# A streaming encoder step on one core: token parts stored straight and read with a stride of eight, the last scatter cut in two, and three waits loosened

## The chip, the cores and the metric

The kernel runs on one core of one Trainium2 chip. A time is the device time of one execution in microseconds (us). The core has TensorE (PE; its loads of stationary operands are shown as PEld), VectorE (DVE), ScalarE (ACT), GpSimd (POOL) and SyncE (SP), which issues most of the DMAs. Each engine works through its own list in order and meets the others at semaphores.

## The reference, cut to what matters

One step of a trunk of two layers, for 256 prompt tokens and 32 new tokens (288 in all) of 1024 features. Of a layer, this change touches the ends and the expert part:

```
z = x @ w_in                                   # rnn stream, q, k, v, two gates
...                                            # recurrence, banded attention, merge
x = LayerNorm(alpha * x + merged @ w_out)
eidx, gate = _route(x2, w_router, e_bias)      # 8 of 64 experts for each token
shared = (silu(x2 @ ws1) * (x2 @ ws3)) @ ws2
ff = shared + sum over chosen experts of gate * (silu(x2 @ w1[e]) * (x2 @ w3[e])) @ w2[e]
x = LayerNorm(alpha * x + ff)
```

Everything is in float32.

## The kernel before

Activations lie transposed in `xT` (feature on the partition, 8 chunks `c` or `k` of 128 features, 288 tokens along the row). Tokens in rows lie in `tok` (three tiles `t` of 128, 128 and 32 tokens, 1024 features along the row). Weights stream in pieces of 1 MB through the ring `dense` (three places); for most of them ACT stores a rounded high part (`high_parts`, fp32r) and DVE the remainder (`low_parts`), and PE adds three products (`over_parts`).

**Start.** SP loads the identity, the tokens, the other constants (743 KB, `consts_in`) and then the first pieces; POOL loads the cached keys and values at once. PE turns the tokens (`fill_xT`, L578 and L581), ACT and DVE copy the chunks to `xT` (even chunks ACT, odd ones DVE, counted by `z_free`), PE turns the tables of small vectors and cached keys (L612, L613), DVE keeps them (L1275 to L1287), ACT takes an exponential (L1026). Only then the first columns of `z` follow (`over_features`, L551, columns m = 0 and 1 in plain float32, then `over_parts` for m = 2 on). PE waits for all eight chunks of `xT` ahead of the first of them, in both layers (L623).

**Router.** After the first LayerNorm PE turns the rows back (L578), ACT and DVE apply scale and shift on the way to `xT` (`norm_back`, L1019 and L1378), PE makes the router's logits (L797), DVE copies them (L1575), PE turns them (L801), and a long chain of small DVE instructions picks the experts (`sel`, L1610). Between these, the token rows are split for the gather: ACT stores the rounded part `xh` (`keep_high`, L1162), DVE the remainder `xl` (`keep_low`, L1568). Both are written in another order than `tok` has: feature f*8+k goes to place k*128+f, so that the gather reads 128 neighbouring words.

**Experts.** They are taken four at a time, a quad, 16 quads a layer, in two halves `u`. `gather` (L849, L850, L852) makes the tokens of a quad into columns: for each chunk k it takes 128 features of `xh` or `xl` as the stationary operand and the one-hot matrix `oh` (256 columns) as the moving one. `up` is L867, `turn` L875, `slots_to_tokens` L896, `down` L887. `combine` (L908, L909) scatters the results back to the tokens, 8 chunks c, each over both halves u; the chunks rotate through the four PSUM banks `SWAP`, and DVE adds each to `ffT` (`add_output`, L1668), which frees its bank. The scatter of a quad runs inside the next quad; that of the last quad has nothing to run in and follows its `down`. Then come three matmuls that only keep the clock up (`keep_clock(2, 3)`, L599), a read of the number of rounds (L946), the turn of `ffT` into rows (`to_tokens`, L586) and the second LayerNorm (`stats` on DVE, L1333; `norm_rows` on ACT, L1010).

A second round of quads would run if an expert had more than 64 tokens; it is skipped here.

The lines that set the reading order of the gather's stationary operand, and the order of the store:

```python
x = slice(k * P, k * P + P)                                        # L842
mm(o, xh[:, t, x], oh[:, t, :], start=t == 0, stop=False)          # L849
activation(xh[0:n, t, :].rearrange("p (k f) -> p f k", k=KC),      # L1162
           tok[0:n, t, :].rearrange("p (f k) -> p f k", k=KC), ACT.Copy)
```

## Time and profile before

| | us |
|---|---|
| median of 3 runs | 1642.45 |
| lowest and highest | 1642.26, 1644.33 |
| the profiled execution | 1643.55 |
| its span in the trace | 1641.7 |
| mean granted TensorE clock in it | 0.992 |

The page gives the busy time of each engine over the span. In 40 equal slices TensorE is at 9 tenths in nearly all of them, the granted clock is 9 or more in all, and the DMA engines are busy for 9 tenths in the slices of the expert part. Below, a row of the timeline reads: start in us from the span's beginning, duration in us (of all instructions of the row), engine, line, operation, written tile and read tiles, shapes, count, and in brackets the idle time ahead of it with what ended it.

### The profile page before, as it was taken

Reading aid. Unit: us, or ns where it says so; the run is one execution under the profiler, and the core shown is the slowest. Engines: PE = TensorE matmul, PEld = TensorE weight load, DVE = VectorE, ACT = ScalarE, POOL = GpSimd, SP = SyncE. Lnnn points to the kernel's source line nnn. Section 1 sums busy time; section 2 is a strip of 40 time slices with the busy share of each in tenths; the row PEclk is TensorE's granted clock in tenths of the full one; section 3 lists DMA queues with packets and bytes.
Section 4 is the critical chain, followed back from the end, with each engine's and each line's share of the span. In section 5 each row is a group of like instructions: output and inputs, shape, how many; then the busy total and the mean of one; then the engine's idle time right before and its main releaser. Section 6 shows DMA issues by size and latency. Waiting matters only on the chain.

```text
span 1641.7 us, 25658 instructions
## 1 busy us (share of the span) xinstructions
PE 1588.7 (97%) x9526; PEld 1050.1 (64%) x9526; DVE 742.4 (45%) x1525; ACT 575.6 (35%) x1138; POOL 23.0 (1%) x38
## 2 busy tenths in 40 slices
PE   7989998999999999999999999989999999999997
PEld 6968997655554555545588789965545555455553
DVE  5568666333323423333464786562333332342335
ACT  4756533232232223223157564342223223222222
POOL 2000000000000000000010000000000000000000
PEclk9999999999999999999999999999999999999999
DMA  7553356399999999999435534457999999999980
GB/s 203 187 185 120 109 174 237 144 369 405 405 391 404 406 391 410 391 401 401 161 105 173 201 104 136 154 205 282 390 403 397 399 401 390 411 394 399 404 355 30
DMA packets 141556, 477.35 MB, mean 291 GB/s; under 512 B 10020, under 2 KB 74084, under 8 KB 108724
## 3 DMA queue, kind: packets, MB, share of 16 engines
q1 hardware_dynamic: 139728, 473.50, 74.7%
q0 software_dynamic: 1408, 2.85, 0.7%
q8 instruction: 42, 0.69, 0.2%
q14 instruction: 22, 0.18, 0.0%
q10 hardware_dynamic: 356, 0.13, 0.0%
HBM read 474.88 MB, written 1.57 MB: 290 GB/s over the span
## 4 chain that ended last, share of the span: by engine, by line
PE 93%; DVE 3%; ACT 1%; issue 1%; DMA 1%; SPq 0%; DVEq 0%; ACTq 0%
PE ps L867 27%; PE ps L887 14%; PE ps L551 7%; PE ps L564 6%; PE ps L566 6%; PE ps L565 6%; PE ps L908 5%; PE ps L909 4%; PE ps L849 4%; PE ps L850 4%; PE ps L852 2%; PE ps L896 1%; PE ps L829 1%; PE ps L875 1%; PE ps L651 1%
## 5 line engine op out<-in xcount | busy, mean ns | idle before, releaser
L867 PE MATMUL ps<-experts,xg 128*64 128x512 f32 x2048 | 450.5, 592 | 0.0
L867 PEld LDWEIGHTS ps<-experts,xg 128*64 128x64 f32 x2048 | 147.5, 137 | 290.9 <-issue 290.1
L887 PE MATMUL ps<-experts,hidT 128*64 128x512 f32 x1024 | 233.8, 598 | 1.8 <-ACT hidT L1200 1.8
L564 PE MATMUL ps<-parts 128*128 128x288 f32 x736 | 222.7, 303 | 0.3
L566 PE MATMUL ps<-parts,dense_lo 128*128 128x288 f32 x736 | 216.6, 294 | 0.0
L1649 DVE TENSOR_TENSOR hid<-ps,hid 128x256 f32<-128x256 f32 x64 | 27.2, 425 | 385.5 <-ACT hid L1194 385.5
L1208 ACT ACTIVATE yh<-ps,gsl 128x512 fp32r<-128x512 f32 x128 | 88.0, 687 | 228.2 <-PE ps L887 228.2
L1194 ACT ACTIVATE hid<-ps 128x256 f32<-128x256 f32 x64 | 24.6, 384 | 397.6 <-PE ps L867 397.6
L1661 DVE SCALAR_TENSOR_TENSOR yl<-ps,gsl,yh 128x512 fp32r<-128x512 f32 x128 | 96.1, 751 | 124.5 <-ACT yh L1208 124.5
L1186 ACT ACTIVATE xg<-ps,gperm_all 128x256 f32<-128x256 f32 x256 | 130.6, 560 | 61.2 <-PE ps L852 57.6
L908 PE MATMUL ps<-ohT,yh 128*128 128x288 f32 x512 | 145.1, 308 | 3.1 <-DVE yl L1661 3.1
L887 PEld LDWEIGHTS ps<-experts,hidT 128*64 128x64 f32 x1024 | 68.5, 136 | 121.6 <-issue 121.6
L564 PEld LDWEIGHTS ps<-parts 128*128 128x128 f32 x736 | 138.1, 188 | 3.7 <-issue 2.0
L909 PE MATMUL ps<-ohT,yl 128*128 128x288 f32 x512 | 139.9, 297 | 0.0
L849 PE MATMUL ps<-oh,xh 128*128 128x256 f32 x512 | 139.3, 294 | 0.0
L566 PEld LDWEIGHTS ps<-parts,dense_lo 128*128 128x128 f32 x736 | 138.5, 188 | 0.0
L850 PE MATMUL ps<-oh,xl 128*128 128x256 f32 x512 | 133.2, 282 | 0.0
L551 PE MATMUL ps<-xT,dense 128*128 128x288 f32 x480 | 128.0, 427 | 3.0 <-ACT xT L1019 1.8
L1668 DVE TENSOR_TENSOR ffT<-ps,ffT 128x288 f32<-128x288 f32 x256 | 115.5, 457 | 24.9 <-PE ps L909 10.5
L1326 DVE TENSOR_TENSOR dense_lo<-dense,parts 128x1024 fp32r<-128x1024 f32 x92 | 108.4, 1220 | 24.7 <-ACT parts L995 24.7
L908 PEld LDWEIGHTS ps<-ohT,yh 128*128 128x128 f32 x512 | 96.2, 188 | 29.2 <-issue 24.3
L551 PEld LDWEIGHTS ps<-xT,dense 128*128 128x128 f32 x480 | 94.9, 200 | 30.9 <-issue 2.1
(275 smaller groups left out, 2022.5 us busy)
## 6 DMA issues: line engine op xcount, KB each, us to landing
experts<-in_w SPq DMA_DIRECT2D x384, 1024.0 KB, 9.6
dense<-in_w_in SPq DMA_DIRECT2D x34, 1024.0 KB, 5.5
dense<-in_w_br_rnn SPq DMA_DIRECT2D x8, 1024.0 KB, 5.3
dense<-in_w_br_attn SPq DMA_DIRECT2D x8, 1024.0 KB, 5.2
dense<-in_w_out SPq DMA_DIRECT2D x8, 1024.0 KB, 5.4
dense<-in_ws SPq DMA_DIRECT2D x6, 1024.0 KB, 5.5
tok<-in_x_prompt SPq DMA_DIRECT2D x1, 1024.0 KB, 5.9
out_y_prompt<-tok SPq DMA_DIRECT2D x2, 512.0 KB, 2.6
```

Source lines behind the costliest of these rows:

```text
L551: last = mm(bank[:, 0:n], w[:, k, col:col + P], rhs(k), start=k == 0, stop=k == KC - 1)
L564: mm(bank[:, 0:T], w_hi[:, k, col:col + P], hi[:, k, :], start=k == 0, stop=False)
L566: last = mm(bank[:, 0:T], w_lo[:, k, col:col + P], hi[:, k, :], start=False, stop=k == KC - 1)
L849: mm(o, xh[:, t, x], oh[:, t, :], start=t == 0, stop=False)
L850: mm(o, xl[:, t, x], oh[:, t, :], start=False, stop=False)
L867: last = mm(ps[e % 2 * CAP:(e % 2 + 1) * CAP, 2, :], xg[:, k, e * CAP:e * CAP + CAP], experts[:, e, 0:2, k * DE:k * DE + DE], start=k == 0 ...
L887: last = mm(ps[e % 2 * CAP:(e % 2 + 1) * CAP, 3 + b, :], hidT[:, m, e % 2 * CAP:(e % 2 + 1) * CAP], experts[:, e, 2, m * D + b * 512:m * D ...
L908: mm(o, yh[:, u, c * P:c * P + P], ohT[:, u, :], start=u == 0, stop=False)
L909: last = mm(o, yl[:, u, c * P:c * P + P], ohT[:, u, :], start=False, stop=u == 1)
L1186: last = activation(xg[:, k, :], ps[:, SWAP[j], k % 2 * 256:k % 2 * 256 + 256], ACT.Identity, bias=gperm_all[:, L, 1, k:k + 1], scale=gper ...
L1326: V.tensor_tensor(low[:, x], slot[:, x], as_f(whi[:, f % 2, x]), ALU.subtract).then_inc(wlo_ready, 1)
L1668: V.tensor_tensor(ffT[:, c, :], ps[:, SWAP[c % len(SWAP)], 0:T], ffT[:, c, :], ALU.add).then_inc(c_added, 1)
```

## The change

Five things:

1. **Stores and reads of the split token rows.** `xh` and `xl` are stored in the order of `tok`; the gather takes every eighth word of a row as its stationary operand, `slice(k, D, KC)`.
2. **Router stage.** DVE itself stores `xh` of tile 0 and its remainder ahead of `norm_back`; the remainders of tiles 1 and 2 are taken after the gate values and after the first one-hot matrix. `oh` moves in memory, so that it doesn't lie on `tok`.
3. **Last quad.** Its scatter is cut: half 0 runs in that quad, where another quad has its gather (chunks 0 to 3 ahead of `turn`, 4 to 7 behind it), half 1 after its `down`. DVE adds 8 + 8 chunks in place of 8. The three matmuls that kept the clock are gone, and the number of rounds is read ahead of the last quad. `to_tokens` starts when four chunks are added.
4. **Start.** The other constants are loaded behind the first weight piece, POOL's loads wait for the tokens, and the tables are turned after columns m = 0 and 1.
5. **First columns of `z`, both layers.** PE waits chunk by chunk for `xT`.

```diff
@@ SP, POOL
-            sp.dma_start(cst[:, P:NCONST], inp["consts"][:, P:NCONST]).then_inc(consts_in, 16)
...
                     load_piece(L, d)
+                    if L == 0 and d == 0:
+                        sp.dma_start(cst[:, P:NCONST], inp["consts"][:, P:NCONST]).then_inc(consts_in, 16)
...
+            pool.wait_ge(x_in, 32)
@@ PE
+                def xk_filled(k):
+                    pe.wait_ge(z_free[k % 2], Z_FIRST + L * Z_HALF - KC // 2 + k // 2 + 1)
+                    return xT[:, k, :]
...
-                        over_features(bank_of(L, Z_RNN + m), D_IN, m % 2 * P, xk, T).then_inc(z_ready[m % 2], 1)
+                        over_features(bank_of(L, Z_RNN + m), D_IN, m % 2 * P, xk if m else xk_filled, T).then_inc(z_ready[m % 2], 1)
+                        if L == 0 and m == 1:
+                            turn_tables()
...
-                            x = slice(k * P, k * P + P)
+                            x = slice(k, D, KC)
...
+                def combine_first(n, cs):
...
+                    for c in cs:
+                        if c < len(SWAP):
+                            pe.wait_ge(c_added, FREE + n * KC)
+                        else:
+                            pe.wait_ge(first_half_added, before + (c - len(SWAP) + 1))
+                        combine_half(0, c).then_inc(first_half_full, 1)
...
                     up(n, 1)
-                    if not last:
+                    if last:
+                        combine_first(n, range(0, 4))
+                    else:
                         gather(n + 1, n, range(2))
                     turn(n, 1)
-                    if not last:
+                    if last:
+                        combine_first(n, range(4, KC))
+                    else:
                         gather(n + 1, n, range(2, 4))
...
-                keep_clock(2, 3)
...
-                to_tokens(ffT)
+                n = pe.snap(done)
+                combine_second(n)
+                to_tokens(ffT, lambda h: pe.wait_ge(c_added, FREE + n * KC + 4 * (h + 1)))
@@ ACT
-                    activation(xh[0:n, t, :].rearrange("p (k f) -> p f k", k=KC),
-                               tok[0:n, t, :].rearrange("p (f k) -> p f k", k=KC), ACT.Copy).then_inc(xh_ready, 1)
+                    activation(xh[0:n, t, :], tok[0:n, t, :], ACT.Copy).then_inc(xh_ready, 1)
...
-                keep_high(0)
+                act.wait_ge(xh_ready, L * NT + 1)
@@ DVE
+                    V.tensor_tensor(low, tok[0:n, t, :], xh[0:n, t, :].bitcast(F32), ALU.subtract).then_inc(xl_ready, 1)
...
+                dve.wait_ge(tok_act, 2 * L * NT + 1)
+                V.tensor_copy(xh[:, 0, :], tok[:, 0, :]).then_inc(xh_ready, 1)
                 keep_low(0)
+                norm_back(L, V_G1, V_B1, Z_FILL1)
...
                     hidden(n, 1)
+                    if last:
+                        add_first(n)
                     keep_turned(n, 1)
```

On PE at the start (the first number after the line is the shape of the result or of the moving operand). Before:

```order
L578 MATMUL ps<-cst,tok 128x128 x16
L581 MATMUL ps<-cst,tok 128x32 x8
L612 MATMUL ps<-cst,B 128x128
L613 MATMUL ps<-cst,B 128x128
L612 MATMUL ps<-cst,B 128x128
L613 MATMUL ps<-cst,B 128x128
L551 MATMUL ps<-xT,dense 128x288 x16
```

After:

```order
L582 MATMUL ps<-cst,tok 128x128 x16
L585 MATMUL ps<-cst,tok 128x32 x8
L555 MATMUL ps<-xT,dense 128x288 x16
L619 MATMUL ps<-cst,B 128x128
L620 MATMUL ps<-cst,B 128x128
L619 MATMUL ps<-cst,B 128x128
L620 MATMUL ps<-cst,B 128x128
```

The two columns of `z` (L555) now stand ahead of the four transposes of the tables (L619, L620).

On PE in the last quad, from `up` of half 1 on. Before, `turn`, `slots_to_tokens` and `down` follow at once, and the whole scatter stands behind them (the first of its rows):

```order
L867 MATMUL ps<-experts,xg 64x512 x16
L873 REGISTER_ALU
L875 MATMUL ps<-cst,hid 128x128 x2
L896 MATMUL ps<-cst,og 128x128 x3
L881 ISA
L887 MATMUL ps<-experts,hidT 64x512 x8
```

After, the last two chunks of half 0's scatter and what follows them:

```order
L938 REGISTER_ALU
L926 MATMUL ps<-ohT,yh 128x288
L927 MATMUL ps<-ohT,yl 128x288
L938 REGISTER_ALU
L926 MATMUL ps<-ohT,yh 128x288
L927 MATMUL ps<-ohT,yl 128x288
L908 MATMUL ps<-cst,og 128x128 x3
L893 ISA
L899 MATMUL ps<-experts,hidT 64x512 x8
```

The matmuls of half 0 (L926, L927) now stand between `up` and `down`; `down` (L899) and the transposes for it (L908) have moved behind them.

On DVE in the router stage, from the memset of unused rows on. Before:

```order
L1561 MEMSET xh 64x1024
L1378 TENSOR_SCALAR xT<-ps,prm_all 128x288 x4
L1568 TENSOR_TENSOR xl<-tok,xh 128x128x8
L1575 COPY ffT<-ps 128x288
L1568 TENSOR_TENSOR xl<-tok,xh 128x128x8
L1579 COPY gsp<-cst 128x3x4
```

After:

```order
L1610 MEMSET xh 64x1024
L1618 CAST xh<-tok 128x1024
L1615 TENSOR_TENSOR xl<-tok,xh 128x1024
L1424 TENSOR_SCALAR xT<-ps,prm_all 128x288 x4
L1623 COPY ffT<-ps 128x288
L1626 COPY gsp<-cst 128x3x4
```

A store of `xh` is new on DVE and stands with the first remainder ahead of `norm_back`; the copy of the logits (L1623) follows `norm_back` directly.

## Rows read from the trace of the kernel before

**Rows 1.** The page, part 1: busy us, share, count of each engine.

```profile
PE 1588.7 (97%) x9526; PEld 1050.1 (64%) x9526; DVE 742.4 (45%) x1525; ACT 575.6 (35%) x1138; POOL 23.0 (1%) x38
```

**Rows 2.** Busy time in one quad: window, length, engines, granted clock, DMA share, GB/s.

```profile
338.44:370.40 31.96, 31.96 (x182) 17.10 (x180) 10.66 (x20) 8.69 (x17) 0.00 (x0) 1.00 0.98 382
```

**Rows 3.** Groups by line and form, PE and PEld: busy us, mean ns, idle before.

```profile
L849 PE MATMUL ps<-oh,xh 128*128 128x256 f32 x512 | 139.3, 294 | 0.0
L850 PE MATMUL ps<-oh,xl 128*128 128x256 f32 x512 | 133.2, 282 | 0.0
L852 PE MATMUL ps<-oh,xh 128*128 128x256 f32 x256 | 72.5, 283 | 0.0
...
L867 PEld LDWEIGHTS ps<-experts,xg 128*64 128x64 f32 x2048 | 147.5, 137 | 290.9 <-issue 290.1 <-ACT xg L1186 0.6
...
L849 PEld LDWEIGHTS ps<-oh,xh 128*128 128x128 f32 x512 | 97.6, 191 | 24.4 <-issue 24.3
```

**Rows 4.** Timeline of PE in a gather, the first and the last of 18 rows.

```profile
361.09 0.27 PE L849 MATMUL ps<-oh,xh 128*128 128x256 f32 x1
...
363.11 0.28 PE L852 MATMUL ps<-oh,xh 128*128 128x256 f32 x1
```

**Rows 5.** Groups by line and form: stores in another order, and straight ones.

```profile
L995 ACT ACTIVATE parts<-dense 128x1024 fp32r<-128x1024 f32 x92 | 92.1, 1052 | 58.0 <-PE ps L566 37.3 <-DMA dense<-in_w_in 15.6 <-DMA dense<-in_w_out 4.4
L1162 ACT ACTIVATE xh<-tok 128x1024 fp32r<-128x1024 f32 x4 | 7.4, 1953 | 0.0
...
L1568 DVE TENSOR_TENSOR xl<-tok,xh 128x1024 fp32r<-128x1024 f32 x4 | 7.7, 1919 | 3.6 <-ACT xh L1162 3.6
```

**Rows 6.** Single lines of DVE, duration ns lowest/median/highest.

```profile
L1326 DVE TENSOR_TENSOR dense_lo<-dense,parts x92: 1204/1219/1227, 21.1 to 1058.1; 128x1024 fp32r<-128x1024 f32 x92
...
L1587 DVE TENSOR_TENSOR gsp<-m x2: 201/201/201, 281.7 to 1089.6; 128x24 f32<-128x24 f32 x2
...
L1595 DVE TENSOR_SCALAR gm<-gs x2: 178/178/178, 283.3 to 1091.2; 128x24 f32<-128x24 f32 x2
```

**Rows 7.** Timeline: loads for transposes at the start, eight in a row.

```profile
12.21 0.57 PEld L581 LDWEIGHTS ps<-cst,tok 32*128 32x128 f32 x8 [0.17 <-issue]
```

**Rows 8.** Timeline of the start: columns of z, and the parts they need.

```profile
16.03 10.94 PE L551 MATMUL ps<-xT,dense 128*128 128x288 f32 x32 [1.15 <-DMA dense<-in_w_in]
...
23.89 2.00 ACT L995 ACTIVATE parts<-dense 128x1024 fp32r<-128x1024 f32 x2 [2.51 <-DMA dense<-in_w_in]
...
28.50 2.35 DVE L1326 TENSOR_TENSOR dense_lo<-dense,parts 128x1024 fp32r<-128x1024 f32 x2
```

**Rows 9.** Timeline at the start of layer 1.

```profile
827.39 2.04 ACT L1019 ACTIVATE xT<-ps,prm_all 128x288 f32<-128x288 f32 x4 [2.23 <-PE ps L581]
...
829.58 2.87 PE L551 MATMUL ps<-xT,dense 128*128 128x288 f32 x8 [1.80 <-ACT xT L1019]
```

**Rows 10.** Timeline of the router stage, layer 1.

```profile
1076.60 0.91 DVE L1561 MEMSET xh<- 64x1024 f32 x1 [0.27 <-issue]
...
1079.34 2.03 DVE L1378 TENSOR_SCALAR xT<-ps,prm_all 128x288 f32<-128x288 f32 x4 [1.83 <-PE ps L581]
...
1083.18 1.92 DVE L1568 TENSOR_TENSOR xl<-tok,xh 128x1024 fp32r<-128x1024 f32 x1 [1.81 <-ACT xh L1162]
...
1085.51 0.89 PE L801 MATMUL ps<-fold,ffT 128*128 128x64 f32 x6 [3.34 <-DVE ffT L1575]
```

**Rows 11.** Timeline of the end of layer 0's experts.

```profile
802.00 0.42 DVE L1649 TENSOR_TENSOR hid<-ps,hid 128x256 f32<-128x256 f32 x1 [5.81 <-ACT hid L1194]
...
803.64 3.65 PE L887 MATMUL ps<-experts,hidT 128*64 128x512 f32 x16 [0.40 <-ACT hidT L1200]
...
808.86 0.40 PE L908 MATMUL ps<-ohT,yh 128*128 128x288 f32 x1 [1.57 <-DVE yl L1661]
...
809.70 4.19 DVE L1668 TENSOR_TENSOR ffT<-ps,ffT 128x288 f32<-128x288 f32 x8 [0.90 <-PE ps L909]
...
816.50 2.83 PE L586 MATMUL ps<-cst,ffT 128*128 128x128 f32 x24 [0.53 <-issue]
```

More of the change, by code:

```diff
@@ L910, in combine, with combine_half, combine_second @@
                         last.then_inc(c_full, 1)
+                def combine_half(u, c):
+                    o = ps[:, SWAP[c % len(SWAP)], 0:T]
+                    mm(o, yh[:, u, c * P:c * P + P], ohT[:, u, :], start=True, stop=False)
+                    return mm(o, yl[:, u, c * P:c * P + P], ohT[:, u, :], start=False, stop=True)
+                def combine_first(n, cs):
+                    before = pe.snap(halves)
+                    pe.wait_ge(ohT_ready, FREE + n * 2 + 1)
+                    pe.wait_ge(yl_ready, FREE + n * 4 + 2)
+                    for c in cs:
[4 more added lines that the diff above has]
+                        combine_half(0, c).then_inc(first_half_full, 1)
+                def combine_second(n):
+                    added = pe.snap(halves)
+                    pe.wait_ge(ohT_ready, FREE + n * 2 + 2)
+                    pe.wait_ge(yl_ready, FREE + n * 4 + 4)
+                    pe.wait_ge(first_half_added, added)
+                    for c in range(KC):
+                        if c >= len(SWAP):
+                            pe.wait_ge(c_added, FREE + n * KC + (c - len(SWAP) + 1))
+                        combine_half(1, c).then_inc(c_full, 1)
                 def quad(n, first=False, last=False):
@@ L1035, in _ @@
                     high_parts(0, 0)
+                    act.wait_ge(neg_abs, 1)
+                    activation(small[:, 0, :, :], small[:, 0, :, :], ACT.Exp).then_inc(exp_abs, 1)
+                    act.wait_ge(rows_kept, 4)
                 high_parts(L, 1)
@@ L1662, in low_part, with add_first, add_second @@
                                                ALU.mult, ALU.subtract).then_inc(yl_ready, 1)
+                def add_first(n):
+                    before = dve.snap(halves)
+                    dve.wait_ge(c_added, FREE + n * KC)
+                    for c in range(KC):
+                        dve.wait_ge(first_half_full, before + (c + 1))
+                        V.tensor_tensor(ffT[:, c, :], ps[:, SWAP[c % len(SWAP)], 0:T], ffT[:, c, :], ALU.add)\
+                            .then_inc(first_half_added, 1)
+                def add_second(n):
+                    dve.wait_ge(first_half_added, dve.snap(halves))
+                    for c in range(KC):
+                        dve.wait_ge(c_full, FREE + n * KC + (c + 1))
+                        V.tensor_tensor(ffT[:, c, :], ps[:, SWAP[c % len(SWAP)], 0:T], ffT[:, c, :], ALU.add).then_inc(c_added, 1)
                 def add_output(n):
```

120 lines of the change are left out of this document (63 added, 57 removed).

## The prediction

> **What bounds the kernel now.** I read the page first, then the busy time of one quad, then the groups by line, then the timeline at the four places that the change touches. The page shows PE busy for 1588.7 us, 97% of the span [rows 1]. In a quad PE is busy in all of its 31.96 us, at full granted clock, while DVE and ACT work 10.66 and 8.69 us [rows 2]: in the expert part (32 quads, over 1000 us of the span) whatever one matmul of PE gains or loses is gained or lost in full, and what DVE or ACT gain there is worth nothing. The DMA engines are at 0.98 there too [rows 2], so a faster PE would soon meet them; a slower one doesn't. Outside the quads PE has gaps, and there the chain through ACT and DVE counts. Parts 2 to 5 of the change work on such gaps. Part 1 touches PE in every quad.
>
> **Part 1, the gather's loads.** The gather has 512 + 512 + 256 = 1280 matmuls [rows 3], 40 in a quad. 18 of them start from 361.09 to 363.11 us [rows 4], so one comes every 2.02 / 17 = 119 ns. Each has its own load of 128 columns. How long can a load be before it sets the pace? A load of 64 columns lasts 137 ns and one of 128 columns 191 ns [rows 3], so 64 columns more take 54 ns, and 128 of them occupy the load path for about 108 ns. It is hidden with only 11 ns to spare.
>
> No row shows PE loading with a stride, so the price is bounded by the nearest rows. On ACT a store of 1024 words per partition takes 1052 ns straight and 1953 ns in the other order [rows 5]: 0.88 ns more for each word. On DVE it is 1219 ns [rows 6] against 1919 [rows 5], 0.68 ns a word. Both write, and jump 128 words. The one read with a jump of exactly eight words is small: L1587 reads 24 pairs so and takes 201 ns, where an instruction on 24 neighbouring words takes 178 [rows 6]; that is 0.96 ns a word, with an operation that isn't the same. Three rows, two engines, and each makes a jumping word 0.7 to 1.0 ns dearer. I take ACT's 0.88, the one between. A load then costs 108 + 128 x 0.88 = 221 ns; it no longer fits under 119 ns, and the gather goes at the pace of its loads: 102 ns more for each of 1280, 131 us. Low end within this case: 0.68 gives 195 ns, +76 ns, 97 us. High end: 0.96 gives 231 ns, and if the 11 ns of today's slack stay as a handover, +123 ns, 158 us. The lowest bound of all is nothing (below, first rival).
>
> The rule of the Trainium skill that speaks against this part stands in "Advanced Engine Details and Errata", section "SBUF Cachelines": lines of 16 bytes, at least two hits in a line needed to hide the memory's latency, a penalty if each access has a line of its own. With fp32 words at a stride of 32 bytes every access has its own. The stores of [rows 5] agree with it in direction; for PE's reads no run here shows it.
>
> A second page is harsher: "Vector Engine (DVE) Microarchitecture Reference", section 5.2, gives 2.50 ns a word for both sources stepping 24 words, against 1.05 straight. An estimate with that figure for PE: 320 ns a load, 201 ns more than today, 257 us in all; I do not use it.
>
> **Part 2, router stage.** DVE reaches the copy of the logits late: `norm_back` ends at 1079.34 + 2.03 = 1081.4 us, but the remainder of tile 0 stands ahead of the copy, waits 1.81 us for ACT's store and lasts until 1085.1, and PE turns the logits at 1085.51 [rows 10]. After the change the store and the remainder are ahead of `norm_back`. DVE is free for them from 1076.60 + 0.91 = 1077.5 [rows 10]; a straight remainder is 1.22 us [rows 6], a straight store about the same, so they end at about 1079.9, 0.55 us later than `norm_back` started. This 0.55 us passes on to the logits and their copy, which now can start right behind: PE would turn the logits at about 1083.3, 2.2 us earlier. The later remainders lie under the 9 us of shared-expert matmuls that follow on PE. Two layers: **-4.4 us**. If the store of DVE is twice as fast, -5.4; if a cold clock eats a part, -3.
>
> **Part 3, the last quad.** The scatter of a half has 16 matmuls, the whole one 32. Half 0 goes into gaps that PE has between `up` and `down`. But its eight additions go to DVE behind `hidden`, which ends at 802.42 [rows 11], at 4.19 / 8 = 0.52 us each [rows 11], and the chunks 4 to 7 on PE wait for the banks that these free. The last of them is on PE at about 804.9, so with the transposes behind it `down` starts at about 805.3 in place of 803.64 [rows 11]: **1.6 us later**, and everything behind it too. Then it comes back. Before, the second scatter started at 808.86, the additions ran from 809.70 to 813.9, and the transposes of `ffT` only started at 816.50 [rows 11], behind the clock matmuls and the read of the rounds: 2.6 us after the last addition. After: scatter of half 1 at 810.5, first addition 0.6 later (two matmuls in place of four), last one done at 815.3, and the transposes of the first four chunks are done by then. Those that are left start at 815.3, and DVE, which was ready for its statistics long before PE was, starts them then: some 1.7 us before today's time. Two layers: **-3.4 us**, bounds 0 (if the branch over the second round costs DVE or PE what the clock matmuls hid) and -5. The clock matmuls' cover goes: PE then works half of the time for 5 us, and if the granted clock fell to the 1.2 GHz level for the 24 transposes that would cost up to 2.8 us each time [rows 11].
>
> **Part 4, start.** The first columns start at 16.03, when the first piece has landed [rows 8]. Without 743 KB ahead of it the piece comes 3 to 4 us earlier, and the tokens are there; so PE may start at about 12.2. But the tables now come behind the columns, and from them a chain hangs: tables (0.65 us), DVE's copies to ACT's exponential (1.8), ACT's next high parts (2.0, which were ready from 23.89 [rows 8]), first tap, DVE's taps (1.6), its low parts (28.50 today [rows 8]). By this chain the low parts for m = 4 would be half done at about 31.5, 1.5 us before PE asks for them today (33.0), and those for m = 6 at about 38.8 against 39.4. What comes out is **-1 us**, between +0.6 and -2. The chain, not the load, is late next. POOL's loads start behind the tokens and are wanted only after the columns, 10 us later.
>
> **Part 5, chunk by chunk.** In layer 1 PE waits for the whole `xT`, from 827.39 (first copy) to 829.58 [rows 9]. With one chunk after 0.57 us it starts at 828.05, and a pair of matmuls takes no less than a copy: **-1.5 us**, at least 0.
>
> **The sum.** Parts 2 to 5: -4.4 - 3.4 - 1.0 - 1.5 = -10.3 us. Part 1: +131. The profiled execution took 1643.55 us around its span of 1641.7, 1.1 above the median of 1642.45, and I count from the median: 1642.45 - 10.3 + 131 = **1763 us**.
>
> **The rivals.** *The stride is free, and the kernel gets faster.* [Rows 7] speak for it: eight loads of 128 columns, for transposes, in 0.57 us; with 0.14 for the last one's own length that is 61 ns apart. So the read port can bring 128 words in 61 ns, while the gather's loads take 108: if a stride only halves what the port brings, a load needs 122 ns, just about today's 119. Up to about 120 ns a load costs nothing; from there each ns is 1.28 us. Against it: on ACT and DVE the price is a time per word, much the same on two engines of different straight pace, which looks like the memory rather than the engine. Time: 1642.45 - 10.3 = 1632 us. The same skill, in "TensorE: Matmul & The Clock Gate", section "Weight-path perf modes", lists "packed or strided" as read pattern of its fast load, which fp32 does not get; it gives no price.
>
> *A small price.* Loads of 125 to 190 ns: 1640 to 1725 us.
>
> *Free stride, but the ends don't pay.* The half scatter holds up `down` by 1.6 us and the late tables hold up m = 4; if the branch and the tables eat what is won, parts 3 and 4 come to nothing or to a loss of 3 us, and parts 2 and 5 leave 1636 to 1640 us. That is also what a change that doesn't do what it says would look like.
>
> **How the numbers follow.** Dear loads, 1729 to 1790 us, 1763 as likeliest: 50%. Small price: 8%. Free stride with the gains: 38%. Free stride, ends don't pay: 4%. The forecast is the first, and its own range is 1729 to 1790. Since the free case has more than 2 in 10, the range over all reaches from it to the high end: 1629 to 1792. Faster by over 0.2% (3.3 us, about what a measurement of this kernel can tell from no change): 38% and half of the 4%, so 0.40; within 0.2%: 0.02; slower: the dear loads and the small price, 0.58.
>
> **What would show it.** Right: matmuls of the gather every 195 to 231 ns in place of 119, loads of about 300 ns where 191 stood, a quad of 35 to 37 us in place of 31.96, DMA share in a quad below 0.95. Wrong: gather still at 119 to 122 ns; then the whole time is the sum of parts 2 to 5. For these: logits turned 2.2 us earlier counted from the memset; `down` of the last quad 1.6 us later after `hidden`, but statistics 1.7 us earlier; first columns at about 12.2; first column of layer 1 0.6 us behind the first copy. A granted clock below full in the quads or a PE that waits for DMA there would break the sum in another way.

## The result, and the profile after

| | us | ratio to before, 95% |
|---|---|---|
| before, median of 4 runs beside it | 1643.39 (1642.26 to 1645.24) | |
| after, median of 4 runs | 1779.45 (1777.47 to 1781.07) | 1.0826, 1.0807 to 1.0845 |

The changed kernel is 136 us slower. The forecast was 1763 us in a range of 1629 to 1792; its case (dear loads) is the one that came, and that case's own range, 1729 to 1790, holds the time. The time is 16 us above the figure called likeliest.

The profile after, part 1 of the page (answers to [rows 1]): PE is busy for 149 us more, and its loads for 153 us more.

```profile
PE 1738.1 (98%) x9514; PEld 1203.2 (68%) x9514; DVE 743.9 (42%) x1543; ACT 568.2 (32%) x1136; POOL 23.1 (1%) x38
```

Busy time over one period of the quads, from one `down` (L887 before, L899 after) to the same one of the next quad; columns as in [rows 2]. First before, then after:

```profile
338.27:369.75 31.48, 31.48 (x180) 16.95 (x178) 10.66 (x20) 8.26 (x16) 0.00 (x0) 1.00 0.98 382
```

```profile
399.97:436.32 36.35, 36.35 (x180) 21.82 (x179) 10.66 (x20) 8.27 (x16) 0.00 (x0) 1.00 0.88 347
```

The same 180 matmuls take 4.87 us more at the same full clock, DVE's and ACT's work is unchanged, and the DMA share has fallen from 0.98 to 0.88. (The 31.96 us of [rows 2] are a stretch that is a little longer than one period; the period is 31.48 us.)

Groups by line and form of after, for [rows 3], and the timeline of a gather, for [rows 4]:

```profile
L861 PE MATMUL ps<-oh,xh 128*128 128x256 f32 x512 | 213.1, 416 | 0.0
...
L862 PEld LDWEIGHTS ps<-oh,xl 128*128 128x128 f32 x512 | 173.1, 338 | 0.0
L861 PEld LDWEIGHTS ps<-oh,xh 128*128 128x128 f32 x512 | 171.3, 335 | 24.4 <-issue 24.3
```

```profile
400.56 0.40 PE L861 MATMUL ps<-oh,xh 128*128 128x256 f32 x1
...
404.67 0.40 PE L864 MATMUL ps<-oh,xh 128*128 128x256 f32 x1
```

A load lasts 335 ns in place of 191. From 400.56 to 404.67 lie 17 steps: 241 ns each in place of 119. 122 ns x 1280 = 156 us, which is 32 times the 4.87 us of a quad. The net loss is 136 us, so the other four parts together brought back about 20 us, twice what I had summed.

Where these came from, by timelines of after. The router stage of layer 0 ([rows 10] has layer 1 before):

```profile
266.44 0.91 DVE L1610 MEMSET xh<- 64x1024 f32 x1 [0.27 <-issue]
...
267.36 0.69 DVE L1618 CAST xh<-tok 128x1024 fp32r<-128x1024 f32 x1
268.09 1.23 DVE L1615 TENSOR_TENSOR xl<-tok,xh 128x1024 fp32r<-128x1024 f32 x1
...
269.23 2.03 DVE L1424 TENSOR_SCALAR xT<-ps,prm_all 128x288 f32<-128x288 f32 x4
...
272.56 0.89 PE L813 MATMUL ps<-fold,ffT 128*128 128x64 f32 x6 [0.55 <-DVE ffT L1623]
```

PE turns the logits 6.12 us after the memset began; before it was 1085.51 - 1076.60 = 8.91 [rows 10], and 8.91 in layer 0 too. The end of layer 0's experts (answers to [rows 11]):

```profile
873.01 0.42 DVE L1696 TENSOR_TENSOR hid<-ps,hid 128x256 f32<-128x256 f32 x1 [5.81 <-ACT hid L1238]
...
873.36 3.00 DVE L1716 TENSOR_TENSOR ffT<-ps,ffT 128x288 f32<-128x288 f32 x8
...
875.75 3.65 PE L899 MATMUL ps<-experts,hidT 128*64 128x512 f32 x16
```

```profile
881.54 3.01 DVE L1723 TENSOR_TENSOR ffT<-ps,ffT 128x288 f32<-128x288 f32 x8 [0.62 <-PE ps L927]
...
884.61 2.40 PE L590 MATMUL ps<-cst,ffT 128*128 128x128 f32 x20 [0.49 <-DVE ffT L1723]
```

`down` starts 2.74 us after `hidden` began, before 1.64: 1.1 us later. The last transposes end at 887.01, 14.0 us after `hidden`; before at 819.33 - 802.00 = 17.3: 3.3 us gained. Last, the first columns of `z`, in both layers (answers to [rows 8] and [rows 9]), and at the start also the first matmul that needs the low parts of the weights, with its wait:

```profile
12.73 9.71 PE L555 MATMUL ps<-xT,dense 128*128 128x288 f32 x32
...
31.03 0.40 PE L568 MATMUL ps<-parts 128*128 128x288 f32 x1 [1.75 <-DVE dense_lo L1372]
```

```profile
895.71 8.00 PE L555 MATMUL ps<-xT,dense 128*128 128x288 f32 x32 [0.34 <-ACT xT L1064]
```

### The profile page after: what moved, and what is told of

Read it like the earlier page. It is cut to its first block, busy times and chain, and to the rows that moved or that the text cites. A ratio compares the mean times of both kernels' runs of the same rounds, so it can differ in the third digit from the quotient of the medians.

```text
span 1779.3 us, 25685 instructions
## 1 busy us (share of the span) xinstructions
PE 1738.1 (98%) x9514; PEld 1203.2 (68%) x9514; DVE 743.9 (42%) x1543; ACT 568.2 (32%) x1136; POOL 23.1 (1%) x38
## 4 chain that ended last, share of the span: by engine, by line
PE 94%; DVE 3%; ACT 1%; issue 1%; DMA 0%; SPq 0%; DVEq 0%; ACTq 0%
PE ps L879 25%; PE ps L899 13%; PE ps L861 7%; PE ps L862 7%; PE ps L555 6%; PE ps L568 5%; PE ps L570 5%; PE ps L569 5%; PE ps L920 4%; PE ps L921 4%; PE ps L864 3%; PE ps L908 1%; PE ps L841 1%; PE ps L887 1%; PE ps L663 1%
## 5 line engine op out<-in xcount | busy, mean ns | idle before, releaser
L879 PE MATMUL ps<-experts,xg 128*64 128x512 f32 x2048 | 450.5, 592 | 0.0
L899 PE MATMUL ps<-experts,hidT 128*64 128x512 f32 x1024 | 233.8, 598 | 1.0 <-ACT hidT L1244 1.0
L861 PE MATMUL ps<-oh,xh 128*128 128x256 f32 x512 | 213.1, 416 | 0.0
L862 PE MATMUL ps<-oh,xl 128*128 128x256 f32 x512 | 206.3, 403 | 0.0
L861 PEld LDWEIGHTS ps<-oh,xh 128*128 128x128 f32 x512 | 171.3, 335 | 24.4 <-issue 24.3
L862 PEld LDWEIGHTS ps<-oh,xl 128*128 128x128 f32 x512 | 173.1, 338 | 0.0
L899 PEld LDWEIGHTS ps<-experts,hidT 128*64 128x64 f32 x1024 | 68.2, 136 | 121.1 <-issue 121.1
L1700 DVE TENSOR_REDUCE gsl<-ps 128x1 f32<-128x288 f32 x64 | 29.0, 453 | 288.2 <-PE ps L908 288.2
L920 PE MATMUL ps<-ohT,yh 128*128 128x288 f32 x480 | 136.3, 309 | 0.0
L921 PE MATMUL ps<-ohT,yl 128*128 128x288 f32 x480 | 131.2, 297 | 0.0
L555 PE MATMUL ps<-xT,dense 128*128 128x288 f32 x480 | 125.8, 422 | 1.1 <-ACT B L1125 0.7
```

The lines of the kernel that those rows point to most:

```text
L555: last = mm(bank[:, 0:n], w[:, k, col:col + P], rhs(k), start=k == 0, stop=k == KC - 1)
L862: mm(o, xl[:, t, x], oh[:, t, :], start=False, stop=False)
L879: last = mm(ps[e % 2 * CAP:(e % 2 + 1) * CAP, 2, :], xg[:, k, e * CAP:e * CAP + CAP], experts[:, e, 0:2, k * DE:k * DE + DE], start=k == 0 ...
L899: last = mm(ps[e % 2 * CAP:(e % 2 + 1) * CAP, 3 + b, :], hidT[:, m, e % 2 * CAP:(e % 2 + 1) * CAP], experts[:, e, 2, m * D + b * 512:m * D ...
L920: mm(o, yh[:, u, c * P:c * P + P], ohT[:, u, :], start=u == 0, stop=False)
L921: last = mm(o, yl[:, u, c * P:c * P + P], ohT[:, u, :], start=False, stop=u == 1)
```

## The experiments

All ratios are to the kernel before, from runs on the same chip. An interval is that of a ratio, 95%. "Pace" is the distance between the starts of neighbouring matmuls in the timeline; "record" of a load is the duration that the profile gives for it, which is longer than the time that the load adds to the pace.

### Is the stride the whole cause, and what are parts 2 to 5 worth?

Undoing part 1 in the changed kernel: straight read, and stores in the old order.

```diff
-                            x = slice(k, D, KC)
+                            x = slice(k * P, k * P + P)
...
-                    activation(xh[0:n, t, :], tok[0:n, t, :], ACT.Copy).then_inc(xh_ready, 1)
+                    activation(xh[0:n, t, :].rearrange("p (k f) -> p f k", k=KC),
+                               tok[0:n, t, :].rearrange("p (f k) -> p f k", k=KC), ACT.Copy).then_inc(xh_ready, 1)
```

> The changed kernel with part 1 undone: the token rows are stored in the other order again and the gather reads 128 neighbouring words; parts 2 to 5 stay. If the stride alone made the kernel slower, the gather returns to a matmul every 119 ns and the quad to 31.5 us. The changed kernel's gather has one every 241 ns, so 1280 x 122 ns = 156 us come back: 1779 - 156 = 1623 us, and some 2 to 3 us more for stores that jump again (DVE's store of tile 0 and its remainder ahead of norm_back): about 1626. My prediction's sum for parts 2 to 5 was -10.3 us, which would be 1633. Rival: a part of the 156 us has another cause (the second half of the last scatter, memory moved, DMA waits); then the quad is longer than 31.5 us and the time stays above 1640.

Measured: 1625.72 us, ratio 0.9888 (0.9873 to 0.9904). It beats the kernel before by 18 us, where the forecast's sum for parts 2 to 5 was 10.3. Busy time in one quad of it:

```profile
344.77:376.25 31.48, 31.48 (x180) 16.94 (x179) 10.66 (x21) 8.27 (x16) 0.00 (x0) 1.00 0.98 391
```

The quad is back at exactly 31.48 us. Nothing else in the changed kernel slows the quads.

The other way round, part 1 alone in the kernel before:

```diff
-                            x = slice(k * P, k * P + P)
+                            x = slice(k, D, KC)
...
+                    activation(xh[0:n, t, :], tok[0:n, t, :], ACT.Copy).then_inc(xh_ready, 1)
```

> The kernel before with part 1 alone: straight stores of xh and xl, gather with a stride of eight. If the stride is the whole cause: 1643.4 + 156 - 2 x 1.5 (the remainder of tile 0 on DVE is shorter, and ACT's store of it too) = about 1796 us, gather matmuls every 241 ns, quad 36.3 us. If parts 2 to 5 share in the slowing, this run is below the changed kernel's 1779.

Measured: 1792.51 us, ratio 1.0903 (1.0884 to 1.0921): 149 us lost by the medians and 152.3 by the spans of the profiled runs (1794.0 against 1641.7). The 156 us less the cheaper stores (below, 1.6 us a layer) would be 153; the spans fit, and the medians lie 4 us lower, about as far as the runs of this kernel lie apart (1790.8 to 1795.84). Its router stage, PE:

```profile
275.93 0.89 PE L801 MATMUL ps<-fold,ffT 128*128 128x64 f32 x6 [1.77 <-DVE ffT L1571]
276.74 9.72 PE L551 MATMUL ps<-xT,dense 128*128 128x288 f32 x32
```

Its memset began at 268.58, so straight stores alone bring the logits from 8.91 to 7.35 us behind it: 1.6 us a layer.

### What does a stride cost a load?

The chunk pairs `j` of the gather got a stride each, on lines of their own. The tokens' columns then hold other features, so the result is another one; number and size of the matmuls are the same. Each of these two kernels, and the one of the next section, was run once:

```diff
-                                mm(o, xh[:, t, x], oh[:, t, :], start=t == 0, stop=False)
+                            if j == 0:
...
+                                    mm(o, xh[:, t, k:k + 128:1], oh[:, t, :], start=t == 0, stop=False)
...
+                            elif j == 1:
...
+                                    mm(o, xh[:, t, k:k + 255:2], oh[:, t, :], start=t == 0, stop=False)
```

> The changed kernel with another stride for each pair of chunks in the gather, each on a line of its own: 1, 2, 4 and 8 words (the computation is altered: the tokens' columns hold other features; the work is of the same size). Pace of the matmuls. Theory line (what counts is how many 16-byte lines of four words the 128 words lie in; 241 / 128 = 1.88 ns a line): stride 1 119 ns, stride 2 (64 lines) 120 to 125, strides 4 and 8 (128 lines) 241 both. Theory jump (each word that isn't the neighbour costs the same): 2, 4 and 8 all 241. Theory distance (the price grows with the bytes spanned, 108 + 133 x (s-1)/7): 127, 165, 241. The Trainium skill, page "Advanced Engine Details and Errata", section "SBUF Cachelines", is for the first of these.

> The same with strides of 3, 5, 7 and 16 words (the computation is altered in the same way; the last pair of chunks always starts at the first tile). Theory line: stride 3 (96 lines) 181 ns, 5, 7 and 16 all 241. Theory jump: all four 241. Theory distance: 146, 184, 222, 393. A rival on banks (only even or power-of-two strides collide): 3, 5 and 7 stay at about 120 and 16 is worse than 241.

Groups by line and form, first of strides 8, 4, 2 and 1 (L877, L872, L867, L862), then of 7, 5, 16 and 3 (L872, L867, L877, L862):

```profile
L877 PEld LDWEIGHTS ps<-oh,xh 128*128 128x128 f32 x128 | 43.2, 338 | 0.0
...
L872 PEld LDWEIGHTS ps<-oh,xh 128*128 128x128 f32 x128 | 41.4, 324 | 0.0
...
L867 PEld LDWEIGHTS ps<-oh,xh 128*128 128x128 f32 x128 | 25.3, 198 | 0.0
L862 PEld LDWEIGHTS ps<-oh,xh 128*128 128x128 f32 x128 | 24.1, 188 | 24.4 <-issue 24.3
```

```profile
L872 PEld LDWEIGHTS ps<-oh,xh 128*128 128x128 f32 x128 | 41.4, 323 | 0.0
...
L867 PEld LDWEIGHTS ps<-oh,xh 128*128 128x128 f32 x128 | 40.8, 318 | 0.0
L877 PEld LDWEIGHTS ps<-oh,xh 128*128 128x128 f32 x128 | 40.5, 316 | 0.0
...
L862 PEld LDWEIGHTS ps<-oh,xh 128*128 128x128 f32 x128 | 33.2, 259 | 24.4 <-issue 24.3
```

The paces are read from the timelines; for stride 4, for one, seven steps from 394.97 to 396.60:

```profile
394.97 0.40 PE L872 MATMUL ps<-oh,xh 128*128 128x256 f32 x1
...
396.60 0.40 PE L874 MATMUL ps<-oh,xh 128*128 128x256 f32 x1
```

| stride, words | 1 | 2 | 3 | 4 | 5 | 7 | 8 | 16 |
|---|---|---|---|---|---|---|---|---|
| groups of four words touched | 32 | 64 | 96 | 128 | 128 | 128 | 128 | 128 |
| load, ns | 188 | 198 | 259 | 324 | 318 | 323 | 338 | 316 |
| pace, ns | 119 | 120 | 174 | 233 | 227 | 233 | 241 | 223 |
| pace / groups, ns | | | 1.8 | 1.8 | 1.8 | 1.8 | 1.9 | 1.7 |

The whole times fit. With a straight read and straight stores the changed kernel would take 1779.45 - 156 = 1623.5 us, and each stride has 320 matmuls: (0 + 1 + 114 + 122) x 0.32 = 76 us more make 1699, against the measured 1699.74. For strides of 3, 5, 7 and 16 it is (55 + 108 + 114 + 104) x 0.32 = 122 us, 1745 against 1743.47. What counts is how many groups of four words, 16 bytes, the 128 words lie in. Distance falls (16 words is no dearer than 4), and so do banks (5 and 7 are as dear as 8), and so does "each word that jumps costs the same", for a stride of 2 costs nothing here. The groups don't explain everything: with 128 groups each, the paces still lie between 223 and 241 ns. Nor is a stride of 2 shown to be free in itself. At 1.8 ns a group its 64 groups would take about 115 ns (an estimate), just under the 119 ns that the matmul takes anyway, and its record is 10 ns longer than the straight one; under a shorter matmul it could show, which no run tried. This is the rule that I had cited against the change: the Trainium skill, "Advanced Engine Details and Errata", section "SBUF Cachelines", asks for at least two hits in a line of 16 bytes. The runs agree: two hits in a group cost nothing at this pace, one and a third on average (a stride of 3) make 174 ns, and one makes 223 to 241 ns.

### Do moving operands pay, and is a strided load free under a longer matmul?

In the kernel with the straight read, `oh` is read with strides of 8, 4 and 2 words for chunk pairs 0, 1 and 2, and `up` reads its 64 columns of `xg` at a stride of eight.

```diff
+                                    mm(o, xh[:, t, x], oh[:, t, :].rearrange("p (a b) -> p b a", b=8), start=t == 0, stop=False)
```

> From e1_reordered, where the stationary rows are read straight. In the gather the moving operand oh is read with strides of 8, 4 and 2 words for chunk pairs 0, 1 and 2 and straight for pair 3 (the columns of a tile come in another order, so slots get other tokens), and up reads its stationary 64 columns of xg with a stride of eight (other features): work of the same size. Theory lines for the load only, moving reads too: 1.8 ns a line would make 256 moving columns take 256 x 1.8 = 460 ns at strides 8 and 4, and nothing at 2. Rival: moving operand is read by another path and costs nothing: 119 ns throughout. For up: 64 lines x 1.8 = 115 ns a load is under its matmul's pace of about 220 ns, so up should not slow down although its load record grows from 137 to about 210 ns; if instead any strided load delays its matmul, up's 32 matmuls in a half take more than 7.04 us.

Measured: 1723.68 us. Load and matmul groups of `up`, and the timeline at a moving stride of 2 (eight steps):

```profile
L894 PE MATMUL ps<-experts,xg 128*64 128x512 f32 x2048 | 450.6, 592 | 0.0
L894 PEld LDWEIGHTS ps<-experts,xg 128*64 128x64 f32 x2048 | 208.2, 196 | 234.2 <-issue 233.4 <-ACT xg L1246 0.4
```

```profile
399.27 0.42 PE L873 MATMUL ps<-oh,xl 128*128 128x256 f32 x1
...
401.10 0.41 PE L874 MATMUL ps<-oh,xh 128*128 128x256 f32 x1
```

`up`: loads of 196 ns in place of 137 [rows 3], matmuls unchanged (450.6 us in all, as in the page of after), so the strided load is hidden where the matmul is long enough. The moving operand is no free path: 217, 232 and 229 ns at strides of 8, 4 and 2, against 119 straight. Both theories fall. It is 0.9 ns a column, whether one word lies in a group or two: for moving fp32r columns the rule of the loads doesn't hold. The cause stays open. The reordered operand is also an access pattern of two dimensions in place of one, and no run tells that from the stride.

### What is each of parts 2 to 5 worth?

Each was undone alone in e1_reordered (1625.72 us, ratio 0.9888). First part 2:

```diff
-                dve.wait_ge(tok_act, 2 * L * NT + 1)
...
-                keep_low(0)
                 norm_back(L, V_G1, V_B1, Z_FILL1)
+                keep_low(0)
```

> The changed kernel with the other order of the rows (as e1_reordered, 1625.7 us) and part 2 undone too: DVE does norm_back first, ACT stores tile 0, the remainders stand where they stood before. Theory, from the traces: in e1_reordered PE turns the logits 7.48 us after the memset, in the kernel before 8.91 us, so 1.4 us a layer; and the shared expert's columns behind it ran at full granted clock (8.0 against 9.3 and 9.6 us), so 1.3 to 1.7 us a layer more if the clock fell because of that wait. Together 5.5 to 6: about 1631.5. Rival, my prediction's sizing without the clock: 2 x 1.4 = 2.8, about 1628.5.

Measured: 1631.14 us, ratio 0.9932 (0.9916 to 0.9948): 5.4 us by the medians, 7.2 by the ratios, 4.3 by the spans (1629.2 against 1624.9), around the theory's 5.5 to 6. Busy time behind the logits of layer 0, u2_no_router first, then e1_reordered (the last three columns are granted clock, DMA share, GB/s):

```profile
275.20:294.30 19.10, 19.09 (x81) 15.00 (x81) 14.70 (x69) 4.91 (x7) 0.00 (x0) 0.91 0.36 142
```

```profile
273.70:291.20 17.50, 17.50 (x81) 14.02 (x81) 14.52 (x68) 4.67 (x7) 0.00 (x0) 1.00 0.47 187
```

The logits are 1.5 us later, and the same 81 matmuls behind them take 1.6 us more, at a granted clock of 0.91, so partly at the lower of the two levels (1.2 GHz in place of 2.4). That is 3.1 us a layer. The spans show less, because the profiled run of e1_reordered has a stretch at the lower level at 890 to 900 us that the one of u2_no_router lacks (below).

Part 3, the whole scatter after the last `down` again:

```diff
-                combine_second(n)
-                to_tokens(ffT, lambda h: pe.wait_ge(c_added, FREE + n * KC + 4 * (h + 1)))
+                keep_clock(2, 3)
...
+                pe.wait_ge(c_added, FREE + pe.snap(done) * KC)
+                to_tokens(ffT, lambda h: None)
```

> As e1_reordered (1625.7 us) with part 3 undone: the whole scatter after the last down, the three matmuls for the clock and the read of the rounds behind it, transposes after all eight additions. Theory from the changed kernel's trace: 3.3 us a layer come back, about 1632. My prediction's size (1.7 a layer): 1629. Rival (the half scatter brings nothing, the gain is of the lighter tail elsewhere): 1626.

Measured: 1633.68 us, ratio 0.9936 (0.9923 to 0.9949): 8.0 us by the medians, 8.6 by the spans (1633.5 against 1624.9), of which about 1 us lies at the start, where the tokens landed later in this profiled run. The tail of layer 0:

```profile
805.20 4.19 DVE L1727 TENSOR_TENSOR ffT<-ps,ffT 128x288 f32<-128x288 f32 x8 [0.89 <-PE ps L921]
...
808.73 2.74 PE L605 MATMUL ps<-cst 128*128 128x512 f32 x6
...
812.45 2.84 PE L590 MATMUL ps<-cst,ffT 128*128 128x128 f32 x24 [0.98 <-issue]
```

Additions of the whole scatter stand 0.52 us apart, and so do PE's groups of four matmuls that feed them. From the first gather to the first columns of layer 1 it is 824.07 - 292.2 = 531.9 us, in e1_reordered 819.17 - 291.2 = 528.0: 3.9 us a layer, where 3.3 was expected. From `hidden` to the last transpose it is 17.8 us here and was 17.3 in the kernel before, against 14.0 with the scatter cut, which is the difference between the two figures.

Part 4, the old order at the start (SP, POOL and the tables):

```diff
-                    if L == 0 and d == 0:
-                        sp.dma_start(cst[:, P:NCONST], inp["consts"][:, P:NCONST]).then_inc(consts_in, 16)
...
-            pool.wait_ge(x_in, 32)
...
-                        if L == 0 and m == 1:
-                            turn_tables()
```

> As e1_reordered (1625.7 us) with part 4 undone: the other constants ahead of the first weight piece, POOL's loads at once, tables ahead of the first columns. Predicted was 1 us; the changed kernel's trace has the K column 1.5 us earlier and some 0.8 more by 260 us, where the clock was low in another place. Expected 1627 to 1628. Rival: the cold clock from 15 to 22 us of the start, which the old order has and the new one doesn't, comes back and costs more: 1630.

Measured: 1626.41 us, ratio 0.9892 (0.9875 to 0.9909): 0.7 us, less than this measurement can tell from nothing. The first gather starts 0.9 us later (292.1 against 291.2). The first columns start at 15.7 us here and at 12.0 in e1_reordered, but the new order then makes PE wait 1.75 us for the low parts (as at 31.03 us in the timeline of after), so most of the earlier start is lost again.

Part 5, waiting for the whole `xT`:

```diff
+                for b in range(2):
+                    pe.wait_ge(z_free[b], Z_FIRST + L * Z_HALF)
...
-                        over_features(bank_of(L, Z_RNN + m), D_IN, m % 2 * P, xk if m else xk_filled, T).then_inc(z_ready[m % 2], 1)
+                        over_features(bank_of(L, Z_RNN + m), D_IN, m % 2 * P, xk, T).then_inc(z_ready[m % 2], 1)
```

> As e1_reordered (1625.7 us) with part 5 undone: PE waits for all of xT ahead of the first column. Predicted was 1.5 us (layer 1 alone): 1627.2. The changed kernel's trace shows 1.5 and 1.7 us more for first columns without the low clock: 1629. Rival: at the start too the wait matters (chunks come one by one while PE could begin), 1 us more: 1630.

Measured: 1630.56 us, ratio 0.9917 (0.9903 to 0.9931): 4.8 us by the medians, 3.7 by the spans. The first columns of layer 1, this kernel and then e1_reordered:

```profile
821.21 9.69 PE L555 MATMUL ps<-xT,dense 128*128 128x288 f32 x32 [1.80 <-ACT xT L1063]
```

```profile
819.17 8.00 PE L555 MATMUL ps<-xT,dense 128*128 128x288 f32 x32 [0.34 <-ACT xT L1064]
```

A wait of 1.46 us more, and then 1.69 us more for the same 32 matmuls, at a granted clock of 0.82 against 1.00. At the start PE waits 1.05 us for a chunk of `xT` that it didn't wait for with part 5, but these first columns end only 0.6 us later (22.8 against 22.2).

### Is it the clock that doubles these gains?

In u2_no_router (u2 for short), PE got three or six matmuls that nothing uses, in its wait of 3.35 us for the copied logits:

```diff
+                keep_clock(2, 6)
                 pe.wait_ge(logits_kept, L + 1)
```

> u2_no_router (1631.1 us, ratio to before 0.9932) plus six matmuls on PE ahead of its wait for the copied logits, where it idles 3.35 us; they compute nothing that is used. Theory clock: half of what part 2 gained is not the wait itself but that the clock falls after it: in u2 the 19.1 us behind the logits ran at a mean granted clock of 0.91, in e1_reordered (gap 0.55 us) the same work took 17.5 us at 1.00. With PE kept busy the granted clock stays 1.00 there, the stretch takes 17.5 us although the logits are as late as in u2, and the kernel takes 2 x 1.6 = 3.2 us less than u2: ratio 0.9912. Rival: the 19.1 us have another cause (DMA, banks, DVE working beside it), then the stretch stays at 19 us and the ratio at 0.9932; or the low clock just moves to another stretch, then the stretch is 17.5 us and the ratio hardly better.

Measured: 1631.66 us, ratio 0.9931 (0.9918 to 0.9945). Timeline of PE, layer 0:

```profile
271.01 5.42 PE L605 MATMUL ps<-cst 128*128 128x512 f32 x12
276.27 0.78 PE L814 MATMUL ps<-fold,ffT 128*128 128x64 f32 x6
276.98 8.03 PE L555 MATMUL ps<-xT,dense 128*128 128x288 f32 x32
```

The columns take 8.03 us at full clock; in u2 they took 9.54. The whole kernel is no faster than u2; 0.9912 was expected. But each filler is two passes of 0.45 us, six overrun the gap by about 1.8 us, and that eats it.

And with three in place of six:

```diff
-                keep_clock(2, 6)
+                keep_clock(2, 3)
```

> As u2_clock, with three filler matmuls in place of six. In u2_clock the granted clock behind the logits stayed at 1.00 and shared_up(0) took 8.03 us in place of 9.54, but the six (two passes each, 12 rows of 0.45 us) ran for 5.42 us where PE idled 3.35, and held up the logits by about 1.8 us, so nothing was won: 1631.7 against 1631.1. Three of them take 2.7 us and fit in the gap. Theory clock: the logits are as late as in u2_no_router (8.4 us behind the start of the transposes), the stretch behind them takes 17.5 to 17.6 us, and the kernel takes about 3.2 us less than u2: ratio 0.9912. Rival: 2.7 us of work in a gap of 3.35 is too little, or the low clock comes elsewhere: ratio 0.993.

Measured: 1631.7 us, ratio 0.9923 (0.9911 to 0.9935). PE in layer 0, and the busy time of a stretch in layer 1:

```profile
274.77 0.89 PE L814 MATMUL ps<-fold,ffT 128*128 128x64 f32 x6 [0.64 <-DVE ffT L1625]
275.58 8.03 PE L555 MATMUL ps<-xT,dense 128*128 128x288 f32 x32
```

```profile
890.00:900.00 10.00, 7.71 (x78) 5.54 (x78) 5.95 (x14) 5.73 (x17) 1.06 (x2) 0.66 0.88 322
```

With the logits as late as in u2 the columns are at 8.03 us, in both layers: where the low clock strikes depends on what PE did in the gap before, and the 1.5 us there are shown to be the clock's. The kernel as a whole didn't get the 3.2 us: 1.5 us by the ratios, within their intervals. Two things stand against the gain. `sel` is now waited for (0.2 and 0.5 us). And the low clock stands elsewhere in the profiled run: 0.66 at 890 to 900 us, in u2_clock 0.83, where u2 had 1.00. That need not be the filler's doing, for e1_reordered, which has none, shows it too:

```profile
890.00:900.00 10.00, 8.45 (x87) 6.45 (x88) 6.84 (x17) 6.72 (x19) 1.06 (x2) 0.83 0.83 318
```

Both filler kernels also have a low stretch between 22 and 45 us (0.93 over the 23 us), ahead of the added filler, but their first columns took 8.0 us and u2's 10.1, so that this evens out. The runs of u2_clock3 say the same: five with a mean clock of 0.995 or 0.996 took 1630.37 to 1632.58 us, and the one at 0.998 took 1627.36, about the 1627.9 that was expected. So the clock's share is shown for the stretch. For the sum the rival, that the low clock turns up in another stretch, isn't refuted.

### A version that beats both

Two hits in a group are enough, so the rows can be stored in pairs of words and read at a stride of two.

```diff
-                            x = slice(k * P, k * P + P)
+                            x = slice(k // 2 * 256 + k % 2, k // 2 * 256 + k % 2 + 255, 2)
...
-                    activation(xh[0:n, t, :].rearrange("p (k f) -> p f k", k=KC),
-                               tok[0:n, t, :].rearrange("p (f k) -> p f k", k=KC), ACT.Copy).then_inc(xh_ready, 1)
+                    activation(xh[0:n, t, :].rearrange("p (j f i) -> p f j i", j=4, i=2),
+                               tok[0:n, t, :].rearrange("p (f j i) -> p f j i", j=4, i=2), ACT.Copy).then_inc(xh_ready, 1)
```

> A version that should beat both: as e1_reordered, but the rows are stored so that the gather reads every second word (place (k//2)*256 + 2f + k%2 holds feature 8f+k); two words lie in each 16-byte line, which in e3 cost the gather nothing (119 ns). The stores then move pairs of words. If the stores are cheaper by lines touched too, DVE's store of tile 0 (1.34 us) and remainder (1.94 us) shrink to about 1.0 and 1.6, the logits come 0.7 us earlier a layer: 1624.3 against 1625.7. If a store's price is per jump and not per line, the same: 1625.7. If three free dimensions cost extra, up to 1627.

Measured: 1623.29 us, ratio 0.9882 (0.9867 to 0.9897), the fastest of all. Its loads, and DVE and PE in the router stage:

```profile
L861 PEld LDWEIGHTS ps<-oh,xh 128*128 128x128 f32 x512 | 99.9, 195 | 24.4 <-issue 24.3
```

```profile
266.77 0.72 DVE L1622 CAST xh<-tok 128x1024 fp32r<-128x1024 f32 x1
267.52 1.23 DVE L1616 TENSOR_TENSOR xl<-tok,xh 128x1024 fp32r<-128x1024 f32 x1
...
272.00 0.89 PE L813 MATMUL ps<-fold,ffT 128*128 128x64 f32 x6 [0.55 <-DVE ffT L1628]
```

A pair costs the stores nothing: 0.72 and 1.23 us, as with straight stores in the changed kernel (0.69 and 1.23); single words moved one by one took 1.34 and 1.94 in e1_reordered. That is better than expected (1.0 and 1.6 us, and logits 0.7 us earlier). ACT's store shows the same, 1.12 us in pairs against 1.06 straight and 2.01 word by word. The pairs jump 256 words and the single words 128, and no run tells whether that matters. The logits come 6.16 us behind the memset, against 7.48 there, 1.3 us earlier. The 2.4 us between the two medians of e7_pairs and e1_reordered are what the stages say (1.3 a layer), but the intervals of the two ratios overlap; that it beats the kernel before is beyond them.

## Why the prediction was right, and which terms were off

**Part 1** carried the result, and its path is confirmed: the gather's load was hidden with little to spare (11 ns is my estimate), the stride made it the pace, and all of PE's time there is on the path. The term that was mis-sized is the price of a word. I took ACT's 0.88 ns a word [rows 5] on top of 108 ns; by the measured pace it is (241 - 108) / 128 = 1.04 ns, above even the 0.96 of [rows 6]. The pace came to 241 ns in place of 221, and part 1 to 156 us in place of 131, just under the high end of 158, which had 0.96 and a handover of 11 ns on top and so 242 ns. The form of the price was wrong too. A price for every word that jumps would make a stride of two as dear as one of eight, and it runs at 120 ns. At a stride of eight each word lies alone in its group, as it does in the stores that the price came from, so the two forms can't be told apart there. That a store's figure on another engine came within 20% of PE's was partly luck: the dear side is the single word in a group on each of the three engines, but what a group costs is each engine's own. The other price, an estimate worked out from the Trainium skill's "Vector Engine (DVE) Microarchitecture Reference", section 5.2, was 320 ns a load and 257 us; the measured 241 ns lie far below it.

**Part 2** was -4.4 and comes to -8.8 with the straight stores, by the stages: the logits 2.8 us a layer earlier in place of 2.2, because DVE's store took 0.69 us where I put 1.2, so that `norm_back` wasn't delayed; and 1.6 us a layer of clock behind the shorter gap, which I had weighed only as a loss. Half of the 2.8 comes from storing straight: with the stores in the old order, e1_reordered against u2_no_router, the part is worth 5.4 us by the medians.

**Part 3** was -3.4 and is -6.6 in the changed kernel (3.3 a layer), or -8.0 by undoing it. I charged each addition of DVE 0.52 us, from 4.19 / 8 [rows 11]. But these were paced by PE, which starts a matmul every 0.13 us and had four for each chunk. With two matmuls a chunk DVE adds every 3.01 / 8 = 0.38 us. So `down` is only 1.1 us late and not 1.6, and the second eight additions last 3.0 us and not 4.2: the 1.7 us a layer that were missing. The clock didn't fall in layer 0's tail, though its filler is gone: 1.00 from 873 to 887 us. DVE's first statistics came 11.5 us behind `hidden`, before 15.2 us: 3.7 us earlier, where I had put 1.7.

**Part 4** was -1.0 and is -0.7, with an uncertainty as large. The first columns started at 12.73 (12.2 was said), and the chain through the tables was late next, as said: PE waited 1.75 us for its low parts.

**Part 5** was -1.5 and is -3.7 to -4.8. The wait went from 1.80 to 0.34 us as worked out; again the clock adds 1.7 us, which the 9.69 against 8.00 us of the first columns show (granted clock 0.82 and 1.00), and the start some 0.6.

**The sum.** Parts 2 to 5 gave 20 us in place of 10.3, above all because the work behind a shorter wait was taken at an unchanged clock (parts 2 and 5) and DVE's additions at PE's pace (part 3). Part 1 cost 25 us more than said. The two errors pull against each other, and the 16 us by which the forecast was low are what is left. That is luck, not sizing.

**The rivals.** The free stride would have been 1632; e1_reordered, which comes nearest to it (it has the dearer stores), took 1625.7. It put at 122 ns what a load takes if a stride halves the port's yield from [rows 7]. At a stride of two the pace is 120 ns, but the matmul's own 119 ns hide the load there, so that doesn't confirm it; at eight the pace is 241 ns, twice the 122, which refutes it. Of the signs, the load of about 300 ns was 335, the quad of 35 to 37 us was 36.35, and the DMA share fell to 0.88, below 0.95; the pace, 195 to 231 ns, was missed at 241, since it left out the handover that the high end counts. `down` was 1.1 us later where 1.6 was said.

## What to carry to other kernels

For PE's loads and for the stores of ACT and DVE, strided access was dear where a word is alone in its 16-byte group, not where a row is merely reordered: a layout in pairs gave the cheap store and a load that the matmul hides at once. It doesn't carry over to moving operands, where a stride of two cost as much as one of eight. Before making an operand cheaper to write, look at its reader's slack: here 1.6 us a layer of shorter stores were paid for with 122 ns on each of 640 matmuls, whose load had by estimate 11 ns to spare. And a pace read from a row belongs to the engine that sets it, so a change that feeds it faster has another.

## What the runs showed of the hardware

- With one load of 128 fp32r columns for each matmul of 256, the matmuls come every 223 to 241 ns when each word lies alone in its 16 bytes, every 174 ns at a stride of three, and every 119 to 120 ns at strides of one and two, where the load is hidden.
- Under a matmul of 512 columns a load of 64 columns at a stride of eight cost nothing (450.6 us for 2048 matmuls, 450.5 with the straight read), though its record grows from 137 to 196 ns.
- A matmul whose moving fp32r operand of 256 columns is reordered takes 217 to 232 ns at strides of 8, 4 and 2, and 119 straight; here a stride of two is not free.
- DVE rounds 1024 words to fp32r in 0.69 us straight, 0.72 in pairs, 1.34 word by word; its remainders take 1.22, 1.22 and 1.94 us.
- Behind the router's gap and at the start of layer 1, the next 32 matmuls took 9.3 to 9.7 us (granted clock 0.82 to 0.86) after gaps of PE of 1.77 to 3.35 us, and 8.0 us at 1.00 after gaps of 0.3 to 0.6 us: a gap that looks worth 1.5 us was worth 3. The length of the gap alone doesn't decide it: after the 1.75 us at 31 us and the 1.78 us at 267 us in e1_reordered the clock stayed at 1.00.
